# First norm reordered around its two modulation vectors, and the last two blocks of the recurrence gated one at a time

## The chip, the cores and the metric

The kernel runs on one core of one Trainium2 chip. The metric is the device time of one execution in microseconds (us). The core's engines are TensorE (PE in the profile; PEld is its weight load), VectorE (DVE), ScalarE (ACT), GpSimd (POOL) and SyncE (SP), which here only issues DMAs. The program is written engine by engine, each engine has its own instruction order, and semaphores are the only link between them.

## The reference, cut to what matters

Two stacks of layers run over 512 tokens of width 1024 in float32. The change touches two places: the norm and modulation in front of the first feed-forward block, and the end of the one recurrent block.

```python
def sublayer_input(x, g, mod_j):
    shift, scale, gate = mod_j[:, 0], mod_j[:, 1], mod_j[:, 2]
    h = rmsnorm(x, g) * (1 + scale[:, None, :]) + shift[:, None, :]
    return h, (1 + gate)[:, None, :]
...
    c_act = jax.nn.silu(c)
    for layer in range(DEPTH):
        mod = (c_act @ mod_w[layer] + mod_b[layer]).reshape(B, N_SUB, 3, D_MODEL)
        h, g = sublayer_input(x, norm_g[layer, 0], mod[:, 0])
        x = x + MACARON_W * g * swiglu(h, ffn_w_gu[layer, 0], ffn_w_down[layer, 0])
...
    a = jnp.exp(log_a)
    b = jnp.sqrt(-jnp.expm1(2.0 * log_a)) * (i * xc).astype(jnp.float32)
    _, hs = lax.associative_scan(_lin_rec_combine, (a, b), axis=1)
    y = jax.nn.gelu(gate) * hs.astype(h.dtype)
    return y @ w_out
```

The recurrence has 10 blocks of 128 channels, numbered 0 to 9.

## The kernel before, in words

Activations lie transposed, as `xT` with 8 tiles of 128 channels by 512 tokens. Every float32 product is made of three products of a high and a low part (`COMBOS`), so each weight panel of 128x2048 is loaded raw by a DMA, cast to its high part by ACT (`split_to`, L1385), and its low part is subtracted by DVE (L1953), or by POOL (L2675) for a few panels that are marked so. For the first feed-forward block, stage `f0`, the low part of the gate panel (panel 0) is made by DVE and that of the up panel (panel 1) by POOL. POOL waits for the step `gain f0` before it makes its first one.

**The start of the program.** One DMA queue brings, in this order, `c`, two pieces of `mod_w`, `x` in two halves, two more pieces of `mod_w`, the small tables, four more pieces of `mod_w`, and then the raw weight panels. A piece of `mod_w` is 256 rows of one of the vectors shift (part 0) or scale (part 1); four pieces make a part. `first_sums` multiplies the rows of a piece on DVE with the matching values of silu(c) and adds them, two instructions a piece, into a 128x1024 sum. `first_turn` sums it over its 128 partitions on TensorE: 8 products of 128x128 by one column of ones (L740), each of them two instructions in the trace, since the operands are float32. `biased` adds `mod_b` and evicts the vector (L1941), `gains` makes the gain of the norm out of the scale vector (L1992). Meanwhile TensorE transposes `x` (L1344), ACT copies it to `xT` (L1889) and then squares the token rows with their sums (L1894), `first_spread` on DVE makes 1/rms and puts it on diagonals (L2048), and `broadcast` (L776) spreads it over all partitions of two PSUM banks.

Then `apply` makes the input of the products, for each half h of the tokens and each of 8 channel tiles j: DVE `scaled` (L2115) writes a PSUM tile of bank 0 or 1, ACT makes `h_high` (L1436) with the shift as its bias, DVE makes `h_low` (L2125) in `rest`. `first_products` of TensorE (L806) follows tile by tile.

**Two helpers decide who waits.** `take_pair` hands out PSUM banks in pairs and first waits until whatever `free_pair` noted for the pair is done. A pair number is fixed if `only[0]` is set; otherwise the pairs go round: 0 for `c`, 2, 4, 6, 0 for `x`, 2 for the tables, 4 for the first call of `first_turn`. `fence` waits until all four engines have passed a mark:

```python
        def fence(q, name):
            for engine in ENGINES:
                q.wait_ge(*at("past", name, engine))
...
            def free_pair(b, *done):
                free[b] = free[b + 1] = list(done)
```

`scaled` holds `fence(q, ("norm", name))`. For `f0` the mark of TensorE is set right behind the second `first_turn`, so it stands for the end of that call. `first_bank("f0", 1)` is bank 4, and `norm_bank("f0", h)` are banks 6 and 7.

**The end of the recurrence.** For each pair of blocks DVE makes the input and two scans (L2333, one a block), POOL multiplies both blocks by gelu(gate) in one instruction of 128x1024 (L2742), ACT casts y_high block by block (L1454) and DVE subtracts y_low (L2152). `project_back` of TensorE then runs the panels of `lru_w_out`, 256 columns each; in the first of them blocks 8 and 9 are the last two of 8, with 6 matmuls of 512 columns each. The next panel's high part is cast by ACT behind its last y_high, and its low part is made by DVE behind that.

Of the kernel before, what the change touches and what calls it, by code (L numbers as in the profile page):

```python
# [9 lines left out]
ALU = mybir.AluOpType  # L10
# [3 lines left out]
P = 128  # L14
# [41 lines left out]
def build(nc, t, out):  # L56
    S, D = t["x"].shape[1:]
    KD = D // P
# [16 lines left out]
    with ExitStack() as ctx:  # L75
# [33 lines left out]
        with nc.sbuf_tensor("before_parts", [P, 12 * S], F32), nc.sbuf_tensor("sb_parts", [P, 4, TRI], F32R) as sb_parts:  # L109
# [18 lines left out]
        s_c, s_in, s_tab, s_rope, s_swap, s_out, s_gate_w, s_dup = (sem(n) for n in (  # L128
            "c_loaded", "x_loaded", "tables_loaded", "rope_loaded", "swapped", "stored", "gate_w_loaded", "copied_half"))
# [158 lines left out]

        entries = []
# [89 lines left out]
        first_acc = [mod_acc[:, :], tiles(20 * S, D)]  # L379
# [242 lines left out]
        def tensor(q):  # L622
# [113 lines left out]
            def first_turn(part):  # L736
                b = base_of["mod", 0, 0, part] = take_pair()
                q.wait_ge(*at("first_sum", part))
                for j in range(KD):
                    m = e.matmul(psum[:, b, j:j + 1], first_acc[part][:, j * P:(j + 1) * P], ones[:, 0:1], start=True, stop=True)  # L740
                m.then_inc(*q.up(s_sums, "mod_turned", 0, 0, part))
                free_pair(b, ("mod", 0, 0, part))
# [596 lines left out]
            q.wait_ge(*at("x_in"))  # L1339
# [33 lines left out]
        def scalar(q):  # L1373
# [53 lines left out]
            def apply(name, h, j0=0, j1=KD):  # L1427
                for j in range(j0, j1):
                    hs, tmp = HALF[h], scaled_tile(name, j)
                    q.wait_ge(*at("scaled", name, h, j))  # L1430
                    h_free(q, name, h)
                    shift = shift_of(name, j)
                    if shift is None:
                        e.copy(H[0][:, j, hs], tmp).then_inc(*q.up(s_square, "h_high", name, j, h))  # L1434
                    else:
                        e.activation(H[0][:, j, hs], tmp, ACT.Identity, bias=shift).then_inc(*q.up(s_square, "h_high", name, j, h))  # L1436
# [158 lines left out]
            def rglru():  # L1595
# [297 lines left out]
            for n in range(NT):  # L1893
                e.activation(row_squares[:, n, :], x_rows[:, n, :], ACT.Square, accum_out=row_sums[:, n:n + 1]).then_inc(*q.up(s_act, "row_square", n))  # L1894
            q.wait_ge(*at("vec_turned"))
            e.copy(vec[:, KD:n_vec], psum[:, base_of.get("vec", 0), 0:n_vec - KD]).then_inc(*q.up(s_act, "vec"))
            load_sqrt("f0")
            mean, root = (stats[0][:, 4 * i:4 * i + NT] for i in range(2))
            q.wait_ge(*at("norm_mean", "f0", 0, 0))
            e.activation(root, mean, ACT.Sqrt).then_inc(*q.up(s_square, "norm_root", "f0", 0, 0))  # L1900
# [14 lines left out]
        def vector(q):  # L1915
# [3 lines left out]
            def first_sums(part, kp):  # L1919
                q.wait_ge(*at("first_mods", part * KD // 2 + kp))  # L1920
                q.wait_ge(*at("c_act"))
                acc = first_acc[part]
                for k in range(2):
                    w, c = first_mods[part * KD // 2 + kp][:, k * D:(k + 1) * D], v("c_act", 2 * kp + k)
                    if kp == 0 and k == 0:
# [58 lines left out]
            def gains(name):  # L1984
                if name not in MOD_OF:
                    return
                layer, sub, weight = MOD_OF[name]
                m, o = mods[layer], 3 * sub * KD
                q.wait_ge(*at("mod", layer, sub, 0))
# [47 lines left out]

            def first_spread():

                mean, root, y2 = (stats[0][:, 4 * i:4 * i + NT] for i in range(3))  # L2040
                q.wait_ge(*at("row_square", NT - 1))
                e.tensor_scalar(mean, row_sums, 1.0 / D, EPS, ALU.mult, ALU.add).then_inc(*q.up(s_norm, "norm_mean", "f0", 0, 0))
# [47 lines left out]
            def apply(name, h, j0=0, j1=KD):  # L2090
# [27 lines left out]
                def rest(j):  # L2118
# [5 lines left out]
                    else:  # L2124
                        m = e.scalar_tensor_tensor(H[1][:, j, hs], scaled_tile(name, j), shift, high, ALU.add, ALU.subtract)  # L2125
# [179 lines left out]
            def rglru():  # L2305
# [21 lines left out]
                def scan(n0):  # L2327
# [338 lines left out]
        def gpsimd(q):  # L2666
# [66 lines left out]
            def rglru():  # L2733
                stage = "lru"

                def second(n0):
                    q.wait_ge(*at("lru_is", n0 + 1))
                    q.wait_ge(*at("conv", n0 + 1))
                    e.tensor_tensor(lru_ii, lru_ii, lru_xc[n0 // 2 % 2], ALU.mult).then_inc(*q.up(s_pool, "lru_ix", n0))
                    q.wait_ge(*at("lru_scan", n0 + 1))  # L2740
                    q.wait_ge(*at("gelu", n0))
                    e.tensor_tensor(lru_rr, lru_rr, lru_gelu[n0 // 2 % 2], ALU.mult).then_inc(*q.up(s_pool, "lru_gated", n0))  # L2742
# [148 lines left out]
        def sync(q):  # L2891
# [132 lines left out]
            def load_first(i):  # L3024
                e.dma_start(first_mods[i].rearrange("p (k n) -> p k n", k=2), mod_piece(i)[3]).then_inc(*q.up(s_first[i], "first_mods", i, by=16))
# [4 lines left out]
            for n in range(NT // 2):  # L3030
                e.dma_start(x_rows[:, 2 * n:2 * n + 2, :], t["x"][0, 2 * n * P:(2 * n + 2) * P, :].rearrange("(n p) d -> p n d", p=P)).then_inc(
                    *q.up(s_in, "x_in", by=16))
# [96 lines left out]
```

## Time and profile before

| what | value |
|---|---|
| three runs | 3153.94, 3156.24, 3156.54 us |
| median | 3156.24 us |
| profiled execution, its own time | 3154.35 us |
| its span | 3152.5 us |
| granted TensorE clock over the span | 0.988 of full |
| TensorE busy | 3076.4 us (98%) |
| VectorE, ScalarE, GpSimd busy | 1710.2, 1190.4, 253.2 us |

The span runs from the first to the last instruction of the profiled execution; its own time has 1.85 us more around it. Busy shares are averages over the whole program, and what one place is worth is read from the stretch around it.

### The profile page before, as it was taken

How to read it: one execution, taken by the hardware profiler on the slowest of the kernel's cores; microseconds unless marked ns; L12 is line 12 of the kernel's file. 1: busy time of each engine (PE TensorE's matmuls, PEld its weight loads, DVE VectorE, ACT ScalarE, POOL GpSimd, SP SyncE). 2: the span in 40 equal slices, each digit the busy share in tenths (PEclk: the TensorE clock that was granted, in tenths of full speed). 3: DMA queues.
4: the chain of work that ended last, by engine and by line, in shares of the span. 5: the costliest groups of instructions: out<-in, count | busy, mean ns of one | idle time of the engine just before them, and what ended most of it. 6: DMA issues, size and time to landing. Idle time of an engine off the chain costs nothing.

```text
span 3152.5 us, 38812 instructions
## 1 busy us (share of the span) xinstructions
PE 3076.4 (98%) x16353; PEld 2590.4 (82%) x16353; DVE 1710.2 (54%) x2365; ACT 1190.4 (38%) x1573; POOL 253.2 (8%) x324
## 2 busy tenths in 40 slices
PE   6999999999999999999999999899999999999998
PEld 6888898888888988888788888877777897787788
DVE  6555553245555554326764233569864356986434
ACT  4222246543222322224753132334573233457322
POOL 0000011120000000000210000012220001222000
PEclk8999999999999999999999999999999999999999
DMA  6545421114546353323122232242322224232222
GB/s 235 187 171 195 169 94 54 54 58 148 195 165 208 108 174 128 100 84 114 57 97 94 97 104 87 64 118 83 91 81 80 96 82 122 80 91 81 80 94 74
DMA packets 290150, 354.23 MB, mean 112 GB/s; under 512 B 10506, under 2 KB 264250, under 8 KB 289978
## 3 DMA queue, kind: packets, MB, share of 16 engines
q1 hardware_dynamic: 289978, 351.76, 34.0%
q8 instruction: 130, 2.13, 0.3%
q14 instruction: 42, 0.34, 0.0%
HBM read 336.52 MB, written 2.10 MB: 107 GB/s over the span
## 4 chain that ended last, share of the span: by engine, by line
PE 88%; DVE 7%; ACT 3%; DMA 1%; issue 1%; SPq 0%; POOL 0%; DVEq 0%; ACTq 0%; POOLq 0%
PE psum L689 53%; PE psum L1236 9%; PE psum L848 6%; PE psum L806 3%; PE psum L1327 3%; PE psum L710 2%; PE psum L730 1%; PE psum L946 1%; DVE w_low L1953 1%; DVE psum L2115 1%; PE psum L1154 1%; PE psum L1175 1%; PE psum L655 1%; DVE h_low L2125 1%; PE psum L802 1%
## 5 line engine op out<-in xcount | busy, mean ns | idle before, releaser
L689 PE MATMUL psum<-h_high,w_high 128*128 128x512 f32 (+1 forms) x1936 | 756.6, 391 | 0.6 <-DVE area L2632 0.4
L689 PE MATMUL psum<-h_high,w_low 128*128 128x512 f32 (+1 forms) x1936 | 753.5, 389 | 0.0
L689 PE MATMUL psum<-h_low,w_high 128*128 128x512 f32 (+1 forms) x1936 | 753.4, 389 | 0.0
L1953 DVE TENSOR_TENSOR w_low<-raw,w_high 128x2048 fp32r<-128x2048 f32 (+3 forms) x246 | 547.2, 2235 | 308.6 <-ACT w_high L1385 308.5
L1385 ACT CAST w_high<-raw 128x2048 fp32r<-128x2048 f32 (+4 forms) x254 | 464.6, 1843 | 570.4 <-DMA raw<-in_ffn_w_gu 234.3
L689 PEld LDWEIGHTS psum<-h_high,w_high 128*128 128x128 f32 (+1 forms) x1936 | 362.7, 187 | 79.8 <-ACT area L1708 1.8
L689 PEld LDWEIGHTS psum<-h_high,w_low 128*128 128x128 f32 (+1 forms) x1936 | 362.6, 187 | 76.6
L689 PEld LDWEIGHTS psum<-h_low,w_high 128*128 128x128 f32 (+1 forms) x1936 | 362.7, 187 | 76.2 <-issue 1.0
L2238 DVE TENSOR_TENSOR area<-area,psum 128x512 f32<-128x512 f32 x88 | 60.2, 684 | 340.5 <-PE psum L689 332.2
L689 PE MATMUL psum<-y_high,w_high 128*128 128x512 f32 x592 | 232.4, 393 | 5.6 <-DVE y_low L2152 3.7
L689 PE MATMUL psum<-y_high,w_low 128*128 128x512 f32 x592 | 231.1, 390 | 0.0
L689 PE MATMUL psum<-y_low,w_high 128*128 128x512 f32 x592 | 231.1, 390 | 0.0
L1454 ACT CAST y_high<-area 128x512 fp32r<-128x512 f32 x102 | 62.7, 620 | 435.3 <-DVE area L2238 404.1
L2157 DVE SCALAR_TENSOR_TENSOR xT<-psum,gain_out,xT 128x512 f32<-128x512 f32 (+1 forms) x156 | 90.7, 623 | 196.2 <-PE psum L689 158.0
L1236 PE MATMUL psum<-h_high,w_high 128*128 128x512 f32 x464 | 186.5, 402 | 3.5 <-ACT area L1768 3.5
L1236 PE MATMUL psum<-h_high,w_low 128*128 128x512 f32 x464 | 181.9, 392 | 0.0
L1236 PE MATMUL psum<-h_low,w_high 128*128 128x512 f32 x464 | 181.8, 392 | 0.0
L2675 POOL TENSOR_TENSOR w_low<-raw,w_high 128x2048 fp32r<-128x2048 f32 x8 | 37.0, 4620 | 1789.8 <-ACT w_high L1385 1750.0
L1970 DVE SCALAR_TENSOR_TENSOR mod_acc<-raw,vec,mod_acc 128x1024 f32<-128x1024 f32 x112 | 143.9, 1285 | 59.0 <-DMA raw<-in_mod_w 53.8
L806 PE MATMUL psum<-h_high,w_high 128*128 128x256 f32 x448 | 132.9, 297 | 7.1 <-ACT h_high L1434 2.2
L848 PE MATMUL psum<-y_high,w_high 128*128 128x256 f32 x480 | 138.2, 288 | 0.2
L848 PE MATMUL psum<-y_low,w_high 128*128 128x256 f32 x480 | 136.5, 284 | 0.0
(329 smaller groups left out, 5135.7 us busy)
## 6 DMA issues: line engine op xcount, KB each, us to landing
raw<-in_ffn_w_gu SPq DMA_DIRECT2D x88, 1024.0 KB, 5.8
raw<-in_mod_w SPq DMA_DIRECT2D x64, 1024.0 KB, 4.8
raw<-in_w_in SPq DMA_DIRECT2D x64, 1024.0 KB, 5.2
raw<-in_ffn_w_down SPq DMA_DIRECT2D x32, 1024.0 KB, 7.3
raw<-in_ffn_w_down SPq DMA_DIRECT2D x16, 768.0 KB, 4.8
raw<-in_sb_w_qkv SPq DMA_DIRECT2D x12, 1024.0 KB, 5.1
raw<-in_lru_w_in SPq DMA_DIRECT2D x10, 1024.0 KB, 5.1
raw<-in_w_out SPq DMA_DIRECT2D x8, 1024.0 KB, 5.2
```

The source lines that it names most:

```text
L689: mm = e.matmul(psum[0:width, base + m, :], wv[a][:, at_k, c0:c0 + width], X[b][:, k, :], start=(at_k == 0 and (a, b) == (0, 0)), stop=(at ...
L710: mm = e.matmul(psum[:, base + m, :], wv[a][:, at_k, m * P:(m + 1) * P], X[b][:, k, :], start=(at_k == 0 and (a, b) == COMBOS[0]), stop=(a ...
L806: mm = e.matmul(psum[:, base + m, HALF[h]], wv[a][:, k, m * P:(m + 1) * P], H[b][:, k, HALF[h]], start=first, stop=last)
L848: mm = e.matmul(psum[:, bank, m * S // 2:(m + 1) * S // 2], wv[a][:, at_k, m * P:(m + 1) * P], X[b][:, k, HALF[h]], start=(at_k == 0 and ( ...
L1236: mm = e.matmul(psum[:, bank, :], wv[a][:, k, m * P:(m + 1) * P], H[b][:, k, :], start=first, stop=last)
L1327: mm = e.matmul(psum[:, base + m, :], wv[x][:, k, m * P:(m + 1) * P], Y[y][:, k, :], start=(k == k0 and (x, y) == (0, 0)), stop=(k == k1 - ...
L1385: e.copy(w_high[x % NW][:, :n], raw[raw_at[m]][:, :n]).then_inc(*q.up(s_high, "w_high", x))
L1454: e.copy(Y[0][:, k, :], src).then_inc(*q.up(s_act, "y_high", stage, j))
L1953: e.tensor_tensor(w_low[raw_at[m]][:, :n], raw[raw_at[m]][:, :n], w_high[x % NW][:, :n].bitcast(F32), ALU.subtract).then_inc(*q.up(s_low, ...
L1970: g = e.scalar_tensor_tensor(mod_acc[:, :], w, c, mod_acc[:, :], ALU.mult, ALU.add)
L2157: return e.scalar_tensor_tensor(dst, src, gain_out[:, j:j + 1], dst, ALU.mult, ALU.add)
L2238: e.tensor_tensor(ffn_gated[n % 4], ffn_silu[n % 4], taken_product(up)[:, m, :], ALU.mult).then_inc(*q.up(s_vec, "gated", stage, n))
```

## The change

It has two halves. In the first norm, `FIRST_PARTS = (1, 0)` makes the scale part come first in the loads and sums. ACT squares the token rows before it copies the transposed `x`, with a semaphore of its own for each half of `x`. The first piece of the shift part is no longer summed by DVE: TensorE multiplies its 128x128 blocks directly with silu(c), and the summed rest is added in the same PSUM columns. The broadcasts of 1/rms are issued inside the second `first_turn`, between that piece and the rest. The shift takes bank 4 in place of bank 0. `biased` of the scale moves behind the shift sums, and DVE makes the low part of panel 0 and the shift vector inside `apply`, behind the first two `scaled`. In the recurrence, for blocks 8 and 9 alone, POOL gates block 8 behind its own scan and DVE gates block 9 behind the second scan.

```diff
+        FIRST_PARTS = (1, 0)
...
-        first_acc = [mod_acc[:, :], tiles(20 * S, D)]
+        first_acc = {FIRST_PARTS[0]: mod_acc[:, :], FIRST_PARTS[1]: tiles(20 * S, D)}
...
             def first_turn(part):
                 b = base_of["mod", 0, 0, part] = take_pair()
+                if part == FIRST_PARTS[1]:
+
+                    q.wait_ge(*at("first_mods", KD // 2))
+                    q.wait_ge(*at("c_act"))
+                    for k in range(2):
+                        for j in range(KD):
+                            e.matmul(psum[:, b, j:j + 1], first_mods[KD // 2][:, k * D + j * P:k * D + (j + 1) * P], v("c_act", k), start=(k, j) == (0, 0), stop=False,
+                                     skip_group_check=True)
+                    for h in range(2):
+                        broadcast("f0", h)
                 q.wait_ge(*at("first_sum", part))
                 for j in range(KD):
-                    m = e.matmul(psum[:, b, j:j + 1], first_acc[part][:, j * P:(j + 1) * P], ones[:, 0:1], start=True, stop=True)
+                    m = e.matmul(psum[:, b, j:j + 1], first_acc[part][:, j * P:(j + 1) * P], ones[:, 0:1], start=part == FIRST_PARTS[0], stop=True,
+                                 skip_group_check=True)
...
-            first_turn(0)
+            first_turn(FIRST_PARTS[0])
             for h in range(2):
-                b = norm_bank("f0", h)
-                wait_free(b)
-                broadcast("f0", h)
-            only[0] = 0
-            first_turn(1)
+                wait_free(norm_bank("f0", h))
+            only[0] = first_bank("f0", 1)
+            first_turn(FIRST_PARTS[1])
             only[0] = None
             q.mark("past", ("norm", "f0"), "PE")
...
-                        split_high(stage, n, n % KD, lru_rr[:, m, :], ("lru_gated", n0))
+                        split_high(stage, n, n % KD, lru_rr[:, m, :], ("lru_gated", n))
...
+            for n in range(NT):
+                q.wait_ge(*at("x_in", n // 2))
+                e.activation(row_squares[:, n, :], x_rows[:, n, :], ACT.Square, accum_out=row_sums[:, n:n + 1]).then_inc(*q.up(s_act, "row_square", n))
+            load_sqrt("f0")
+            mean, root = (stats[0][:, 4 * i:4 * i + NT] for i in range(2))
+            q.wait_ge(*at("norm_mean", "f0", 0, 0))
+            e.activation(root, mean, ACT.Sqrt).then_inc(*q.up(s_square, "norm_root", "f0", 0, 0))
             for j in range(1, KD, 2):
                 q.wait_ge(*at("x_turned", j))
...
-                    return [("mod", 0, 0, 1)]
+                    return [("mod", 0, 0, FIRST_PARTS[0])]
...
                 scaled(j0)
+                if (name, h) == ("f0", 0):
+                    scaled(j0 + 1)
+                    split_to(0)
+                    biased(0, 0, FIRST_PARTS[1])
                 for j in range(j0, j1):
                     if j + 1 < j1:
-                        scaled(j + 1)
+                        if (name, h, j) != ("f0", 0, 0):
+                            scaled(j + 1)
...
+                    if n0 == NB - 2:
+                        q.wait_ge(*q.newest)
+                        q.wait_ge(*at("gelu", n0))
+                        e.tensor_tensor(lru_rr[:, 1, :], lru_rr[:, 1, :], lru_gelu[n0 // 2 % 2][:, 1, :], ALU.mult).then_inc(
+                            *q.up(s_vec, "lru_gated", n0 + 1))
...
-            for part in range(2):
-                for kp in range(KD // 2):
-                    first_sums(part, kp)
-                    if (part, kp) == (1, 0):
-                        biased(0, 0, 0)
-                        first_spread()
-            split_to(0)
-            biased(0, 0, 1)
+            gain_part, shift_part = FIRST_PARTS
+            for kp in range(KD // 2):
+                if kp == 3:
+                    first_mean()
+                first_sums(gain_part, kp)
+            first_spread()
+            for kp in range(1, KD // 2):
+                first_sums(shift_part, kp)
+            biased(0, 0, gain_part)
             gains("f0")
             q.mark("past", ("norm", "f0"), "DVE")
             ffn("f0")
...
+                    q.wait_ge(*at("gelu", n0))
+                    if n0 == NB - 2:
+                        q.wait_ge(*at("lru_scan", n0))
+                        e.tensor_tensor(lru_rr[:, 0, :], lru_rr[:, 0, :], lru_gelu[n0 // 2 % 2][:, 0, :], ALU.mult).then_inc(*q.up(s_pool, "lru_gated", n0))
+                        return
                     q.wait_ge(*at("lru_scan", n0 + 1))
```

Left out of the diff are the two semaphores of the halves of `x`, the waits for them, the mean split off `first_spread` as `first_mean`, and the index arithmetic that follows `FIRST_PARTS`. ACT and DVE also wait for the shift vector in `apply` of every modulated norm, where `gains` waited for it before.

## Rows read from the trace of the kernel before

**Rows 1.** The page, part 1: busy time, share of the span, instructions.
```profile
PE 3076.4 (98%) x16353; PEld 2590.4 (82%) x16353; DVE 1710.2 (54%) x2365; ACT 1190.4 (38%) x1573; POOL 253.2 (8%) x324
```
**Rows 2.** The chain that ended last, 0 to 60 us: start, duration, what.
```profile
43.18 16.85 PE psum L806 x125
```
**Rows 3.** The timeline, 0 to 50 us: start, duration, engine, line, what, idle before.
```profile
13.76 6.53 PE L1344 MATMUL psum<-ident,area 128*128 128x128 f32 x32 [11.19 <-DMA area<-in_x]
...
16.30 5.31 DVE L1929 SCALAR_TENSOR_TENSOR mod_acc<-h_plain,vec,mod_acc 128x1024 f32<-128x1024 f32 x4 [5.07 <-DMA h_plain<-in_mod_w]
...
21.23 1.06 ACT L1894 ACTIVATE area<-area 128x1024 f32<-128x1024 f32 x1
...
22.79 0.75 DVE L1926 TENSOR_SCALAR area<-y_plain,vec 128x1024 f32<-128x1024 f32 x1 [1.17 <-DMA y_plain<-in_mod_w]
...
28.93 2.04 PE L776 MATMUL psum<-inv,ones 128*128 128x256 f32 x4 [4.74 <-DVE inv L2048]
29.29 8.03 DVE L1929 SCALAR_TENSOR_TENSOR area<-y_plain,vec,area 128x1024 f32<-128x1024 f32 x6
...
33.48 1.90 ACT L1385 CAST w_high<-raw 128x2048 fp32r<-128x2048 f32 x1 [5.63 <-DMA raw<-in_ffn_w_gu]
...
37.23 2.28 DVE L1953 TENSOR_TENSOR w_low<-raw,w_high 128x2048 fp32r<-128x2048 f32 x1
...
41.04 0.17 DVE L1941 TENSOR_TENSOR mod<-psum,vec 128x8 f32<-128x8 f32 x1 [1.53 <-PE psum L740]
...
41.52 0.88 DVE L2115 SCALAR_TENSOR_TENSOR psum<-xT,gain_in,psum 128x256 f32<-128x256 f32 x2
41.57 4.55 POOL L2675 TENSOR_TENSOR w_low<-raw,w_high 128x2048 fp32r<-128x2048 f32 x1 [39.79 <-DVE gain_in L1992]
42.05 0.87 ACT L1436 ACTIVATE h_high<-psum,mod 128x256 fp32r<-128x256 f32 x2 [3.65 <-DVE psum L2115]
42.55 0.48 DVE L2125 SCALAR_TENSOR_TENSOR h_low<-psum,mod,h_high 128x256 fp32r<-128x256 f32 x1
```
**Rows 4.** Line L740: count, ns min/median/max, first to last start in us.
```profile
L740 PE MATMUL psum<-ones,mod_acc x16: 242/250/352, 21.8 to 23.8; 128*128 128x1 f32 x16
L740 PE MATMUL psum<-ones,area x16: 344/352/353, 37.5 to 40.7; 128*128 128x1 f32 x16
```
**Rows 5.** TensorE by window: length, busy (instructions), granted clock, DMA share, GB/s.
```profile
23.00:23.50 0.50, 0.50 (x5) 0.50 1.15 467
...
38.00:40.00 2.00, 2.00 (x11) 0.50 1.08 386
...
46.00:47.00 1.00, 1.00 (x7) 0.56 0.07 16
...
1613.00:1614.00 1.00, 0.65 (x2) 0.80 0.00 0
```
**Rows 6.** The timeline by engine, 1505 to 1520 us: POOL and DVE.
```profile
1512.32 2.39 POOL L2742 TENSOR_TENSOR area<-area 128x1024 f32<-128x1024 f32 x1 [10.21 <-DVE area L2333]
...
1512.71 4.15 DVE L1953 TENSOR_TENSOR w_low<-raw,w_high 128x2048 fp32r<-128x2048 f32 x1 [0.47 <-ACT w_high L1385]
```
**Rows 7.** The timeline by engine, 1590 to 1640 us: DVE, POOL, ACT, DVE, DVE, PE, PE.
```profile
1607.02 2.34 DVE L2333 TENSOR_TENSOR_SCAN area<-area 128x512 f32<-128x512 f32 x2
...
1609.44 2.34 POOL L2742 TENSOR_TENSOR area<-area 128x1024 f32<-128x1024 f32 x1 [11.68 <-DVE area L2333]
...
1611.86 1.14 ACT L1454 CAST y_high<-area 128x512 fp32r<-128x512 f32 x2 [6.22 <-POOL area L2742]
...
1612.51 1.29 DVE L2152 TENSOR_TENSOR y_low<-area,y_high 128x512 fp32r<-128x512 f32 x2 [3.15 <-ACT y_high L1454]
...
1615.06 4.49 DVE L1953 TENSOR_TENSOR w_low<-raw,w_high 128x2048 fp32r<-128x2048 f32 x2 [1.17 <-ACT w_high L1385]
...
1613.35 0.55 PE L689 MATMUL psum<-y_high,w_high 128*128 128x512 f32 x1 [3.73 <-DVE y_low L2152]
...
1617.78 0.28 PE L848 MATMUL psum<-y_high,w_high 128*128 128x256 f32 x1
```

More of the change, by code:

```diff
@@ L127, in build @@
         s_first = [sem(f"first_mods{i}") for i in range(KD)]
-        s_c, s_in, s_tab, s_rope, s_swap, s_out, s_gate_w, s_dup = (sem(n) for n in (
-            "c_loaded", "x_loaded", "tables_loaded", "rope_loaded", "swapped", "stored", "gate_w_loaded", "copied_half"))
+        s_in = [sem(f"x_loaded{i}") for i in range(NT // 2)]
+        s_c, s_tab, s_rope, s_swap, s_out, s_gate_w, s_dup = (sem(n) for n in (
+            "c_loaded", "tables_loaded", "rope_loaded", "swapped", "stored", "gate_w_loaded", "copied_half"))
         steps, base_of = {}, {}
@@ L1338, in tensor @@
             turn_tables(0, 1, "c_vec")
-            q.wait_ge(*at("x_in"))
+            for n in range(NT // 2):
+                q.wait_ge(*at("x_in", n))
             for j in range(KD):
@@ L1435, in apply @@
                     else:
+                        q.wait_ge(*at("mod", *MOD_OF[name][:2], 0))
                         e.activation(H[0][:, j, hs], tmp, ACT.Identity, bias=shift).then_inc(*q.up(s_square, "h_high", name, j, h))
@@ L1892, in scalar @@
                     q.mark("x", "f0", jj, 1)
-            for n in range(NT):
-                e.activation(row_squares[:, n, :], x_rows[:, n, :], ACT.Square, accum_out=row_sums[:, n:n + 1]).then_inc(*q.up(s_act, "row_square", n))
             q.wait_ge(*at("vec_turned"))
             e.copy(vec[:, KD:n_vec], psum[:, base_of.get("vec", 0), 0:n_vec - KD]).then_inc(*q.up(s_act, "vec"))
[L1897 to L1900, printed above, removed]
             for i, a in enumerate((neg_tri, neg_ones)):
@@ L1919, in first_sums @@
             def first_sums(part, kp):
-                q.wait_ge(*at("first_mods", part * KD // 2 + kp))
+                i = FIRST_PARTS.index(part) * KD // 2 + kp
+                q.wait_ge(*at("first_mods", i))
                 q.wait_ge(*at("c_act"))
@@ L1923, in first_sums @@
                 for k in range(2):
-                    w, c = first_mods[part * KD // 2 + kp][:, k * D:(k + 1) * D], v("c_act", 2 * kp + k)
-                    if kp == 0 and k == 0:
+                    w, c = first_mods[i][:, k * D:(k + 1) * D], v("c_act", 2 * kp + k)
+                    if kp == FIRST_PARTS.index(part) and k == 0:
                         m = e.tensor_scalar(acc, w, c, None, ALU.mult)
@@ L1988, in gains @@
                 m, o = mods[layer], 3 * sub * KD
-                q.wait_ge(*at("mod", layer, sub, 0))
                 q.wait_ge(*at("mod", layer, sub, 1))
@@ L2036, in spread, with first_mean @@
                     m.then_inc(*q.up(s_norm, "norm_diag", name, h, which))
+            def first_mean():
+                mean = stats[0][:, 0:NT]
+                q.wait_ge(*at("row_square", NT - 1))
+                e.tensor_scalar(mean, row_sums, 1.0 / D, EPS, ALU.mult, ALU.add).then_inc(*q.up(s_norm, "norm_mean", "f0", 0, 0))
             def first_spread():
                 mean, root, y2 = (stats[0][:, 4 * i:4 * i + NT] for i in range(3))
-                q.wait_ge(*at("row_square", NT - 1))
-                e.tensor_scalar(mean, row_sums, 1.0 / D, EPS, ALU.mult, ALU.add).then_inc(*q.up(s_norm, "norm_mean", "f0", 0, 0))
                 q.wait_ge(*at("norm_root", "f0", 0, 0))
@@ L2124, in rest @@
                     else:
+                        q.wait_ge(*at("mod", *MOD_OF[name][:2], 0))
                         m = e.scalar_tensor_tensor(H[1][:, j, hs], scaled_tile(name, j), shift, high, ALU.add, ALU.subtract)
@@ L2739, in second @@
                     e.tensor_tensor(lru_ii, lru_ii, lru_xc[n0 // 2 % 2], ALU.mult).then_inc(*q.up(s_pool, "lru_ix", n0))
+                    q.wait_ge(*at("gelu", n0))
[3 more added lines that the diff above has]
+                        return
                     q.wait_ge(*at("lru_scan", n0 + 1))
-                    q.wait_ge(*at("gelu", n0))
-                    e.tensor_tensor(lru_rr, lru_rr, lru_gelu[n0 // 2 % 2], ALU.mult).then_inc(*q.up(s_pool, "lru_gated", n0))
+                    e.tensor_tensor(lru_rr, lru_rr, lru_gelu[n0 // 2 % 2], ALU.mult).then_inc(*q.up(s_pool))
+                    for m in range(2):
+                        q.mark("lru_gated", n0 + m)
                 first_products(stage)
@@ L3024, in load_first @@
             def load_first(i):
-                e.dma_start(first_mods[i].rearrange("p (k n) -> p k n", k=2), mod_piece(i)[3]).then_inc(*q.up(s_first[i], "first_mods", i, by=16))
+                src = mod_piece(FIRST_PARTS[2 * i // KD] * KD // 2 + i % (KD // 2))[3]
+                e.dma_start(first_mods[i].rearrange("p (k n) -> p k n", k=2), src).then_inc(*q.up(s_first[i], "first_mods", i, by=16))
             e.dma_start(t_rows[0:KD, 0, :], t["c"].rearrange("a (n p) -> (a n) p", p=P)).then_inc(*q.up(s_c, "c_in", by=16))
@@ L3031, in sync @@
                 e.dma_start(x_rows[:, 2 * n:2 * n + 2, :], t["x"][0, 2 * n * P:(2 * n + 2) * P, :].rearrange("(n p) d -> p n d", p=P)).then_inc(
-                    *q.up(s_in, "x_in", by=16))
+                    *q.up(s_in[n], "x_in", n, by=16))
             load_first(2)
```

## The prediction, made before the changed kernel ran

> **What bounds the kernel now.** I read the page first: TensorE is busy for 98% of the span [rows 1]. A start of about 43 us and a handful of stalls are all that an edit to the other engines can win, and every microsecond by which TensorE begins its steady work later is a microsecond at the end. Next the chain that ended last, in its first 60 us: the products of stage `f0` enter it at 43.18 and run on without a gap [rows 2]. So the first half of the change is worth whatever it moves that one time by. The timeline shows what ends last there [rows 3]: the shift and scale sums on DVE stop at 37.32, TensorE turns the second vector until 41.0 [rows 4], DVE evicts it at 41.04, scales two tiles from 41.52, and ACT and DVE finish the first h tile at 43.03. The second half of the change touches one stall of 3.73 us, behind the last two blocks of the recurrence [rows 7].
>
> **First half, the sums.** The order of the loads does not change, only which part the pieces hold. The transposes begin at 13.76, when both halves of `x` are there, and a square of 128x1024 takes 1.06 with some 0.2 for its sum, so four end by about 18.7 even if they start only then. The third and fourth piece's sums run from 16.30 to 21.61 [rows 3]. The mean fits between them, the root is ready when they end, and the spread of 1/rms is over by about 23.5. The xT copies come some 2 us later than before, at about 23.4, and nobody asks for them before 40 us. Before, `first_spread` sat in the middle of the shift sums, waiting for ACT, and six sums ran from 29.29 to 37.32 [rows 3]. Now only the loads hold them. The fifth piece landed at 22.79 and the raw gate panel, four loads later, at 33.48 [rows 3], so a load takes 2.67 and the last piece lands at about 30.8. Its two sums of 1.3 each end at 33.4, 3.9 us earlier than before. That is the gain of this half.
>
> **First half, what stands in front of TensorE.** The second `first_turn` begins with `take_pair`. With `only[0]` at `first_bank("f0", 1)` it asks for bank 4, and bank 4 is the one that the round of pairs gave to the scale vector, noted as free when the scale vector is evicted. DVE evicts it (`biased`) only behind all its shift sums, at 33.6. So the product of the first shift piece and the two broadcasts, which are meant to fill the idle TensorE from 24 us on, stand in the queue until 33.7. No row shows banks; this is read from the code.
>
> What then runs on TensorE: the piece has 16 products of a 128x128 block by one column, 32 instructions. In the same form 16 instructions started over 37.5 to 40.7 [rows 4], 0.215 each, so 32 take 6.9, to 40.6. The two broadcasts took 2.04 [rows 3] and end at about 42.6. The turn of the rest is the old 16 instructions, 3.5 [rows 4], and ends at 46.1.
>
> DVE meanwhile has nothing to do. Its next instruction is `scaled`, whose fence asks for TensorE's mark of this norm, and the mark is still set behind the second `first_turn`. So both `scaled` wait until 46.1, not for the broadcast alone. They take 0.88, and then comes `split_to(0)`, the low part of panel 0, 2.28 [rows 3], which before ran at 37.23 beside the turn of the vector and cost nothing. That cover is gone: 46.15 to 47.05, and to 49.35. The shift vector with its small gaps makes 49.6, h_high (0.48) 50.1, h_low (0.48) 50.6, and with the old step of 0.15 to TensorE the first product starts at 50.75, against 43.18 [rows 2]. **The first half costs 7.5 us.** Behind ACT's first h_high stand only the other h_high; behind DVE's wait stand all its low parts, and TensorE waits for both. POOL's low part of the up panel is freed earlier (its wait for the gain ends at 33.8, before at 41.5) and is needed only after 48 products, so it gives nothing. After the start the pace is that of before: h tiles every 0.91 us on DVE, TensorE at half clock at first. From 60 us on TensorE waits for little, and what the DMA queue does next hangs on TensorE's own marks, so I carry the 7.5 to the end.
>
> **The clock in this stretch.** The granted clock was 0.50 (1.2 GHz) from 23.0, in the middle of the first one-column products, through all of the second ones, and rose at about 46.7, some 3.6 us into the dense products of `f0` [rows 5]. So 3.5 us of one-column products did not raise it, and it even fell during such products. I take half clock for all 48 of the new run.
>
> The Trainium skill (TensorE: Matmul & The Clock Gate, Part 1) says that an idle array is clocked at half, and that sustained activity gives the full clock back. It makes no exception for one-column products. By that rule TensorE, busy from 33.7 for 12 us, would be at full clock for most of them. The case that this gives is the second rival.
>
> **Second half, the recurrence.** Before: two scans to 1609.36, POOL's gate of both blocks to 1611.78, y_high of block 8 to 1612.45, y_low of block 8 to 1613.16, TensorE at 1613.35 [rows 7]. Now POOL has half the work, 1.17, and DVE the other half, some 0.68 by its y_low of the same size [rows 7]. POOL could start at 1608.2, behind the first scan. But the second scan runs then, on two SBUF operands. In the one place where such an operation of DVE was issued beside POOL's gate, it took 4.15 in place of 2.28, and ended one normal duration behind POOL's end [rows 6, 3]. So I take the two engines as excluding one another: POOL gates from 1609.4 to 1610.6, DVE's gate of block 9 runs behind it to 1611.25, y_high of block 8 is ready at 1611.2, y_low from 1611.3 to 1611.95, TensorE at 1612.15, 1.2 earlier. The next panel's low part comes 1.15 earlier too (ACT's casts follow its last y_high, 1611.85 against 1613.0), and with it the start at 1617.78 [rows 7]. After its stall of 3.73 TensorE ran at half clock (0.80 granted in the window in which it resumed [rows 5]). With 2.5 us of idle time it may keep the full one for its 12 matmuls, but it would then wait for that low part, so little more comes of it: **1.3 us gained**. Bounds: with no exclusion POOL is done at 1609.4, DVE at 1610.1, y_low of block 8 at 1610.8, and 2.6 are gained. If DVE's gate goes first, POOL ends at 1611.3 and 0.5 are gained.
>
> The Trainium skill (GPSIMD Engine Reference, Key points) states that GpSimd shares its SBUF interfaces with VectorE, and that they contend when the DVE instruction has two SBUF inputs. Rows 6 agree with it. For a scan no row here shows it; without the rule's reach to scans the gain would be nearer 2.6.
>
> **The sum.** +7.5 − 1.3 = +6.2 us. The profiled execution took 3154.35, its span 3152.5 with 1.85 around it, which gives 3160.6. It lies 1.9 below the median of the three runs, 3156.24, and from the median it is 3162.4. I forecast 3162. The nearest runs before lie up to 2.6 us apart, so about 0.2%, 6.3 us, is what a measurement of this kernel can tell from no change, and the forecast lies on that line.
>
> **The rivals.**
>
> 1. *The piece runs early after all*: TensorE is not held at bank 4. For it: it is what the new order is built for, and my reading of the round of pairs has no row behind it. Then the first vector is turned by 24.2, the piece by 31.0, the broadcasts by 33.0, the rest from 33.5 to 37.1, which is 9.0 earlier than in my case. The first half gives −1.5 (the low part of panel 0 and the fence remain), the total is −2.8 us: 3153.4, no slower than before. It decides if the first of the 32 instructions starts before DVE's eviction of the scale. 0.10.
>
> 2. *The long run on TensorE raises the clock*. Against it stand rows 5. The first 3.5 us at half clock hold 16 instructions, to 37.2, the next 16 at half the spacing 1.7, the broadcasts 1.0, the turn 1.75, to 41.7: 4.4 earlier, the first half costs 3.1, the total is +1.8: 3158. 0.13.
>
> 3. *The recurrence gives nothing*: a gate of half the size costs POOL as much as the whole, 2.34 [rows 7], and block 8 is as late as before. Against it: POOL's 128x2048 took 4.55 and its 128x1024 2.34 [rows 3, 7], so it goes by size. The total is then +7.4: 3163.6, slower by 0.23%. It decides as soon as POOL's half takes over 2.2. 0.12.
>
> Something else 0.05; my own case 0.60.
>
> **The numbers.** My case alone: the landing of the last piece may be off by 1 either way, the turn by 0.5, the recurrence is between −2.6 and −0.5, so +4.5 to +8.3, that is 3160.5 to 3164.5. The range for all cases takes in rivals 2 and 3, most of the scatter of the runs and part of rival 1: 3155 to 3165.5. Slower by over 0.2% are nearly half of my case (0.29), most of rival 3 (0.10) and a little of the rest: 0.41. Faster by over 0.2% needs −6.3, which no case gives: 0.03. Within 0.2%: 0.56.
>
> **What would show it.** Right: L740's new 32 instructions start at about 33.7, released by DVE, and the clock stays 0.50; DVE is idle from 34 to 46; its w_low of panel 0 starts at about 47; the first L806 at about 50.7; POOL's gate of block 8 starts at 1.2 to 1.3 us behind the first scan (1609.4 plus the shift), DVE's own gate behind it. Wrong: L740's new instructions at 24 us (rival 1), a clock of 1.00 before 42 us (rival 2), `scaled` before the end of the turn (then I misread the fence, and 3 to 4 us of the cost go), or a later stage whose stall takes the shift up.

## The result, and the profile after

The changed kernel took 3164.01 us (median of ten runs, 3161.4 to 3167.3), the kernel before 3156.59 (ten runs beside it): ratio 1.0024, 95% interval 1.0015 to 1.0033, so it is 0.24% slower, 7.4 us. I had forecast 3162, in a range of 3155 to 3165.5, with 0.41 on slower by over 0.2%. The profiled execution took 3161.87 with a span of 3160.1, against 3154.35 and 3152.5. Line numbers shift by some 13 to 30: L740 is now L752, the new shift piece is L746, L776 is L789, L806 is L819, L1953 is L1968, L2115 is L2132, L2742 is L2772.

The chain that ended last, in its part of the first 60 us, beside [rows 2]:

```profile
24.09 9.56 issue
33.66 6.96 PE psum L746 x32
40.62 1.92 PE psum L789 x4
42.53 3.22 PE psum L752 x16
...
45.94 0.88 DVE psum L2132 x2
46.82 2.19 DVE w_low L1968
...
50.34 11.77 PE psum L819 x77
```

The products of `f0` begin at 50.34 where they began at 43.18. Before them, three blocks of TensorE work stand nose to tail, and before those a hole of 9.56 us. The profile calls it "issue" and names no releaser. By the code, the first thing that TensorE's queue asks for there is the wait in `take_pair` for bank 4, and the bank 2 run below tests that. The timeline of the changed kernel has both sides of the hole, and beside [rows 3] it shows what ran earlier:

```profile
11.52 1.06 ACT L1901 ACTIVATE area<-area 128x1024 f32<-128x1024 f32 x1 [7.24 <-DMA area<-in_x]
...
28.17 5.31 DVE L1944 SCALAR_TENSOR_TENSOR area<-y_plain,vec,area 128x1024 f32<-128x1024 f32 x4 [0.47 <-DMA y_plain<-in_mod_w]
...
33.40 0.16 DVE L1956 TENSOR_TENSOR mod<-psum,vec 128x8 f32<-128x8 f32 x1
...
33.66 6.96 PE L746 MATMUL psum<-vec,y_plain 128*128 128x1 f32 x32 [9.56 <-issue]
...
38.83 4.50 POOL L2704 TENSOR_TENSOR w_low<-raw,w_high 128x2048 fp32r<-128x2048 f32 x1 [37.05 <-ACT w_high L1397]
...
45.94 0.88 DVE L2132 SCALAR_TENSOR_TENSOR psum<-xT,gain_in,psum 128x256 f32<-128x256 f32 x2 [12.19 <-PE psum L752]
46.73 2.28 DVE L1968 TENSOR_TENSOR w_low<-raw,w_high 128x2048 fp32r<-128x2048 f32 x1
```

The sums end at 33.48 instead of 37.32. The shift piece starts 0.1 us behind the end of DVE's eviction of the scale (33.40 and 0.16). DVE is idle for 12.19 us, until the turn (L752) ends. TensorE by window, columns as in [rows 5]:

```profile
34.00:36.00 2.00, 2.00 (x11) 0.50 1.10 347
...
44.00:46.00 2.00, 1.74 (x9) 0.50 0.01 2
...
54.00:56.00 2.00, 2.00 (x13) 0.60 0.00 0
56.00:57.00 1.00, 1.00 (x11) 1.00 0.00 0
```

TensorE is busy from 33.66 to 45.75, all of it at half clock, and the clock rises only at about 55.6, 5.3 us into the dense products, where it took 3.7 before (to 46.9).

The end of the recurrence, beside [rows 7], in the order of the engines DVE, POOL, ACT, PE:

```profile
1614.48 2.34 DVE L2356 TENSOR_TENSOR_SCAN area<-area 128x512 f32<-128x512 f32 x2
1616.86 1.59 DVE L2361 TENSOR_TENSOR area<-area 128x512 f32<-128x512 f32 x1
1618.64 1.29 DVE L2175 TENSOR_TENSOR y_low<-area,y_high 128x512 fp32r<-128x512 f32 x2 [0.19 <-ACT y_high L1467]
...
1621.20 4.49 DVE L1968 TENSOR_TENSOR w_low<-raw,w_high 128x2048 fp32r<-128x2048 f32 x2 [1.19 <-ACT w_high L1397]
...
1615.85 2.05 POOL L2772 TENSOR_TENSOR area<-area 128x512 f32<-128x512 f32 x1 [9.91 <-DVE area L2356]
...
1619.48 0.47 PE L691 MATMUL psum<-y_high,w_high 128*128 128x512 f32 x1 [1.72 <-DVE y_low L2175]
...
1623.64 0.35 PE L861 MATMUL psum<-y_high,w_high 128*128 128x256 f32 x1 [1.19 <-DVE w_low L1968]
```

POOL's half began at 1615.85, behind the first scan, but ended at 1617.90: 1.08 behind the end of the second scan at 1616.82. That start is not the one that I had named as a sign, some 1.2 us behind the end of the first scan. The profile has the instruction as begun and shows the wait inside its 2.05 us, where half of POOL's 2.34 for both blocks would be 1.17. DVE's own gate needed 1.59 in place of some 0.68, and ended 0.55 behind POOL. So the end times say that the two engines took turns. The stall in front of block 8 is 1.72 instead of 3.73, and a new wait of 1.19 for the low part of the next panel follows.

For the lags and leads below I counted the matmuls of two traces back from the last one and compared the starts of matmuls with the same count; a lag says how much later, a lead how much earlier a version does the same work than the kernel before, each in its profiled execution. In the changed kernel the lag behind the kernel before is 7.2 us at the start of `f0`, 7.8 from 60 us on, 8.1 in front of block 8, 5.9 at the next panel, 6.0 at 1900 us, up to 9.2 behind 2000 us, and 7.5 at the end.

### The profile page after: what moved, and what is told of

It reads as the page before. It is cut to its first block, busy times and chain, and to the rows that moved or that the text cites. A ratio compares the mean times of both kernels' runs of the same rounds, so it can differ in the third digit from the quotient of the medians.

```text
span 3160.1 us, 38877 instructions
## 1 busy us (share of the span) xinstructions
PE 3080.6 (97%) x16385; PEld 2595.5 (82%) x16385; DVE 1707.1 (54%) x2364; ACT 1189.8 (38%) x1573; POOL 253.7 (8%) x324
## 4 chain that ended last, share of the span: by engine, by line
PE 87%; DVE 7%; ACT 3%; issue 1%; DMA 1%; SPq 0%; POOL 0%; DVEq 0%; ACTq 0%; POOLq 0%
PE psum L691 53%; PE psum L1249 9%; PE psum L861 6%; PE psum L819 3%; PE psum L1340 3%; PE psum L712 2%; PE psum L732 1%; PE psum L959 1%; DVE w_low L1968 1%; DVE psum L2132 1%; PE psum L1167 1%; PE psum L1188 1%; PE psum L657 1%; DVE h_low L2143 1%; PE psum L815 1%
## 5 line engine op out<-in xcount | busy, mean ns | idle before, releaser
L1968 DVE TENSOR_TENSOR w_low<-raw,w_high 128x2048 fp32r<-128x2048 f32 (+3 forms) x246 | 547.3, 2236 | 309.7 <-ACT w_high L1397 309.7
L1985 DVE SCALAR_TENSOR_TENSOR mod_acc<-raw,vec,mod_acc 128x1024 f32<-128x1024 f32 x112 | 143.8, 1284 | 60.8 <-DMA raw<-in_mod_w 55.6
L819 PE MATMUL psum<-h_high,w_high 128*128 128x256 f32 x448 | 132.9, 297 | 10.4 <-DVE h_low L2143 4.6
```

The lines of the kernel that those rows point to most:

```text
L819: mm = e.matmul(psum[:, base + m, HALF[h]], wv[a][:, k, m * P:(m + 1) * P], H[b][:, k, HALF[h]], start=first, stop=last)
L1968: e.tensor_tensor(w_low[raw_at[m]][:, :n], raw[raw_at[m]][:, :n], w_high[x % NW][:, :n].bitcast(F32), ALU.subtract).then_inc(*q.up(s_low, ...
L1985: g = e.scalar_tensor_tensor(mod_acc[:, :], w, c, mod_acc[:, :], ALU.mult, ALU.add)
```

## The experiments

All are compared with the kernel before, run on the same chip beside them (median 3155.27, then 3155.11).

| run | median, us | runs | ratio, 95% interval | first product of `f0`, us |
|---|---|---|---|---|
| norm_only | 3163.92 | 5 | 1.0032 (1.0020 to 1.0044) | 50.44 |
| recur_only | 3153.82 | 12 | 0.9995 (0.9987 to 1.0004) | 43.49 |
| bank2 | 3155.61 | 11 | 1.0003 (0.9994 to 1.0011) | 42.18 |
| bank2_mark | 3153.91 | 11 | 0.9995 (0.9987 to 1.0004) | 40.48 |
| no_panel | 3158.23 | 10 | 1.0008 (0.9999 to 1.0018) | 47.11 |
| mark_only | 3162.40 | 10 | 1.0020 (1.0011 to 1.0029) | 47.52 |
| warm | 3151.28 | 11 | 0.9983 (0.9974 to 0.9992) | 40.40 |
| best | 3149.78 | 11 | 0.9986 (0.9978 to 0.9995) | 40.52 |

**The first half alone.** The edit puts the recurrence back:

```diff
-                        split_high(stage, n, n % KD, lru_rr[:, m, :], ("lru_gated", n))
+                        split_high(stage, n, n % KD, lru_rr[:, m, :], ("lru_gated", n0))
...
-                    if n0 == NB - 2:
-                        q.wait_ge(*q.newest)
-                        q.wait_ge(*at("gelu", n0))
-                        e.tensor_tensor(lru_rr[:, 1, :], lru_rr[:, 1, :], lru_gelu[n0 // 2 % 2][:, 1, :], ALU.mult).then_inc(
-                            *q.up(s_vec, "lru_gated", n0 + 1))
```

> The first half of the change alone, the recurrence as before. My account: the whole loss is here. First product of f0 at about 50.3 us against 43.2, the stall in front of block 8 of the recurrence back at 3.7 us, the time 7 to 8 us above before. Rival (the loss comes from both halves or from later stages): well under 5 us above before.

It took 8.7 us more than before (6.3 to 13.9 by the interval, from five runs), a little above the 7 to 8 that I expected. The lag is 7.3 at the start of `f0`, 7.4 behind it and 7.0 at 1618. The loss is all in this half. POOL's gate and TensorE behind it:

```profile
1616.46 2.36 POOL L2766 TENSOR_TENSOR area<-area 128x1024 f32<-128x1024 f32 x1 [11.01 <-DVE area L2356]
...
1620.39 0.47 PE L691 MATMUL psum<-y_high,w_high 128*128 128x512 f32 x1 [3.12 <-DVE y_low L2175]
```

The stall is 3.12 here, not 3.7: the first half moved TensorE by 7.7 and DVE only by 7.0 at this point (the scans start at 1614.04 against 1607.02), and the difference came off the stall.

**The second half alone**, the same lines put into the kernel before:

> The second half alone, the first norm as before. My account: POOL's gate of block 8 and DVE's of block 9 exclude each other as in the changed kernel, the stall shrinks from 3.7 to about 2.4 us, full clock behind it, 1.5 to 2.3 us below before; that is under what the time can show, so the trace has to. Rival (the gain of 2.2 us seen in the changed kernel was there only because the first half had shifted TensorE against DVE): 0.5 us or less at the first product of the next panel.

```profile
1608.42 2.04 POOL L2748 TENSOR_TENSOR area<-area 128x512 f32<-128x512 f32 x1 [10.36 <-DVE area L2333]
...
1612.04 0.47 PE L689 MATMUL psum<-y_high,w_high 128*128 128x512 f32 x1 [2.12 <-DVE y_low L2152]
1616.19 0.36 PE L848 MATMUL psum<-y_high,w_high 128*128 128x256 f32 x1 [1.14 <-DVE w_low L1953]
```

TensorE resumes at 1612.04 instead of 1613.35 and reaches the next panel at 1616.19 instead of 1617.78. TensorE ran 0.3 us late before that point, so against its own lag it gained 1.6 and 1.9 us. DVE was not late (its scans start at 1607.05 against 1607.02), and counted from the start of the scans TensorE resumes 1.3 us earlier and reaches the next panel 1.6 us earlier. In the changed kernel the same count gives 1.3 and 1.6 too. So 1.6 of the 2.3 seen there are the half's own and independent of the first half; the rest is the shift between DVE and TensorE seen in norm_only, of which this run has 0.3. The time itself (1.45 us below before) can't tell this from nothing. The rival falls.

**The shift vector in bank 2**, one argument:

```diff
-            only[0] = first_bank("f0", 1)
+            only[0] = first_bank("f0", 0)
```

> The changed kernel with the shift vector in bank 2 in place of bank 4, nothing else. My account: nothing holds the shift piece any more, its 32 instructions start at about 24 to 26 us, the broadcasts end before 33.4, the turn of the rest ends at about 37, both scaled follow at once (the fence still waits for the turn), low part of panel 0 to 40.2, first product at about 41.5: some 9 us earlier than in the changed kernel, 1.5 earlier than before, time some 3 to 4 us below before. Rival (the 32 instructions on TensorE are themselves the cost): first product still behind 48 us.

```profile
24.09 5.82 PE L746 MATMUL psum<-vec,y_plain 128*128 128x1 f32 x32
...
29.77 2.05 PE L789 MATMUL psum<-inv,ones 128*128 128x256 f32 x4
...
37.78 0.88 DVE L2132 SCALAR_TENSOR_TENSOR psum<-xT,gain_in,psum 128x256 f32<-128x256 f32 x2 [3.56 <-PE psum L752]
38.57 2.28 DVE L1968 TENSOR_TENSOR w_low<-raw,w_high 128x2048 fp32r<-128x2048 f32 x1
39.33 5.93 POOL L2704 TENSOR_TENSOR w_low<-raw,w_high 128x2048 fp32r<-128x2048 f32 x1 [37.55 <-ACT w_high L1397]
...
42.18 0.55 PE L819 MATMUL psum<-h_high,w_high 128*128 128x256 f32 x1 [4.61 <-DVE h_low L2143]
```

The same 32 instructions now start at 24.09, and the hole is gone. The first product comes 8.2 us earlier than in the changed kernel. I expected 41.5; in this execution DVE's last sum ended 0.46 later, at 33.94. So bank 4 is the cause of the hole, and the shift piece does not hold up the first product where it stands in TensorE's idle time. `scaled` still waits for the turn (3.56 idle, released by PE). The time is back at that of before and not 3 to 4 below it: the lead is 2.9 us behind the recurrence and turns into a lag of 1.3 by the end. More on that below.

**The mark moved behind the broadcasts**, on top of bank 2:

```diff
                     for h in range(2):
                         broadcast("f0", h)
+                    q.mark("past", ("norm", "f0"), "PE")
...
             only[0] = None
-            q.mark("past", ("norm", "f0"), "PE")
```

> As the bank 2 version, and TensorE's mark of the norm set behind the broadcasts instead of behind the turn of the rest. My account: both scaled start at about 33.7, the low part of panel 0 runs from 35.7 (its high part) to 38.0 beside the turn, ACT's cast of panel 1 ends at 38.7 and holds the first h_high, first product at about 39.8, 1.7 earlier than with the bank alone, time 5 to 6 us below before. Rival (the mark changes nothing, since the shift vector is awaited anyway): first product within 0.5 us of the bank 2 version.

```profile
36.07 0.88 DVE L2132 SCALAR_TENSOR_TENSOR psum<-xT,gain_in,psum 128x256 f32<-128x256 f32 x2 [2.27 <-ACT w_high L1397]
36.86 2.28 DVE L1968 TENSOR_TENSOR w_low<-raw,w_high 128x2048 fp32r<-128x2048 f32 x1
...
40.48 0.55 PE L820 MATMUL psum<-h_high,w_high 128*128 128x256 f32 x1 [3.33 <-DVE h_low L2143]
```

The step was right, 1.7 us between the two versions as expected, but for the size by luck: `scaled` started not at 33.7 but at 36.07, released by ACT's cast of panel 0. ACT has a mark of its own in the same fence, set behind its first `split_to`, which I had not looked at. The lead behind the recurrence is 6.0 us (1.3 of it from a stretch near 450 us in which the clock fell before and did not here), the lead in the medians 1.4, where I had expected 5 to 6.

**The mark alone, with bank 4 kept:**

> The changed kernel with bank 4 kept and only the mark moved behind the broadcasts. My account: the shift piece still starts at 33.7, both scaled start at 42.5 when the broadcast is done, the low part of panel 0 waits for POOL's panel 1 (to 43.4) and ends at 45.6, the shift vector comes at 45.9, first product at about 47.1: 3.2 us earlier than in the changed kernel. Rival (the mark changes nothing, since the shift vector is awaited anyway): 50.

```profile
39.16 4.51 POOL L2704 TENSOR_TENSOR w_low<-raw,w_high 128x2048 fp32r<-128x2048 f32 x1 [37.38 <-ACT w_high L1397]
...
43.07 0.88 DVE L2132 SCALAR_TENSOR_TENSOR psum<-xT,gain_in,psum 128x256 f32<-128x256 f32 x2 [8.98 <-PE psum L790]
43.86 2.28 DVE L1968 TENSOR_TENSOR w_low<-raw,w_high 128x2048 fp32r<-128x2048 f32 x1
...
47.52 0.55 PE L820 MATMUL psum<-h_high,w_high 128*128 128x256 f32 x1 [1.46 <-DVE h_low L2143]
```

`scaled` is now released by the broadcast (L790) and no longer by the turn. The first product lies 2.8 us before that of the changed kernel, 3.2 expected, in an execution in which the shift piece itself started 0.33 late (33.99). Both of the waits that I read from the code are thus shown one by one. The median, 3162.40, is hardly below that of the changed kernel.

**No shift piece on TensorE**, all four pieces on DVE, bank and mark as in the changed kernel:

```diff
-                    q.wait_ge(*at("first_mods", KD // 2))
-                    q.wait_ge(*at("c_act"))
-                    for k in range(2):
-                        for j in range(KD):
-                            e.matmul(psum[:, b, j:j + 1], first_mods[KD // 2][:, k * D + j * P:k * D + (j + 1) * P], v("c_act", k), start=(k, j) == (0, 0), stop=False,
-                                     skip_group_check=True)
...
-            for kp in range(1, KD // 2):
+            for kp in range(KD // 2):
                 first_sums(shift_part, kp)
```

> The changed kernel (bank 4 and the mark as they are) with all four shift pieces summed on DVE and no shift piece on TensorE. DVE has 2 us free before the second shift piece lands, so its sums should still end at about 33.5. My account: the broadcasts start at 33.7 and end at 35.7, the turn ends at 39.1, both scaled follow; then DVE's low part of panel 0 meets POOL's of panel 1, which has run since 38.8. If two such instructions exclude each other it ends near 45.5 and the first product starts at about 47; if not, at 42.2 and 43.6. Rival (the order of the norm is the cost and not the queue in front of TensorE): first product at 50 as in the changed kernel.

```profile
34.12 2.05 PE L782 MATMUL psum<-inv,ones 128*128 128x256 f32 x4 [9.98 <-issue]
...
39.13 4.50 POOL L2697 TENSOR_TENSOR w_low<-raw,w_high 128x2048 fp32r<-128x2048 f32 x1 [37.35 <-ACT w_high L1390]
...
40.37 5.41 DVE L1961 TENSOR_TENSOR w_low<-raw,w_high 128x2048 fp32r<-128x2048 f32 x1
...
47.11 0.55 PE L812 MATMUL psum<-h_high,w_high 128*128 128x256 f32 x1 [7.73 <-DVE h_low L2136]
```

The hole stays without the piece, since the broadcasts stand behind the same wait. DVE's sums end at 33.94, in an execution whose raw panel came 0.3 late, so some 0.2 later than with the piece on TensorE if that is taken off: in the changed kernel DVE was idle for 2.00 us until the next piece landed, and an extra piece takes 2.03. So the shift piece on TensorE buys next to nothing, and in bank 4 it puts 6.9 us more in front of the turn. Only 3.2 of those come back at the first product, because DVE's low part then meets POOL's: 5.41 us for an instruction of 2.28, ending 2.15 behind POOL's end at 43.63. In the bank 2 run, where DVE's instruction came first, it is POOL that pays, 5.93 for 4.55.

**Four dense products in the gap**, on top of bank 2 and the moved mark:

```diff
                 free_pair(b, ("mod", 0, 0, part))
+                if part == FIRST_PARTS[1]:
+                    for i in range(4):
+                        e.matmul(psum[:, b + 1, 0:S // 2], ones[:, :], inv[:, 0:S // 2], start=True, stop=True)
```

> The version with bank 2 and the moved mark, with four extra dense products (128x128 by 256 columns of float32, result never read, no part of the reference's computation is left out) on TensorE behind the turn, in the gap of 3.3 us before the first product. My account: one-column products do not raise the clock and dense ones do, so with these four the clock rises within about 1 us of the first product where it took 3.5 us, the first 17 products run at full clock, and TensorE is then paced by DVE: up to 1.5 us gained behind the first panel half, first product itself at 40.5. Rival (TensorE's being busy is what counts, and it was busy from 24 to 37 in vain): no change of the rise.

Windows without them (first three lines) and with them (last three):

```profile
37.00:39.00 2.00, 0.15 (x1) 0.50 1.10 356
...
41.00:43.00 2.00, 2.00 (x12) 0.50 0.79 315
43.00:44.00 1.00, 1.00 (x6) 0.51 0.02 8
```

```profile
37.00:39.00 2.00, 2.00 (x6) 0.50 1.10 357
39.00:40.00 1.00, 1.00 (x3) 0.51 1.07 394
40.00:41.00 1.00, 0.99 (x7) 1.00 1.04 408
```

The clock rises at about 40.0, 0.4 us before the first product, against 44.0. In both versions TensorE ran the one-column products from 24.5 to 31.4 and from 33.5 to 37.1 and the two broadcasts between them at half clock, and the clock did not rise; with the four dense products behind them it rose 3.1 us after they began. In the run of the next experiment, with the same four products, it rose at about 41.8, 4.9 us after they began and 1.3 behind the first product, so their effect is there but not to the microsecond. The lead is 3.6 against 2.8 at 48 us, less than the 1.5 more that I allowed for, since TensorE now waits for DVE's tiles, and from 60 us on it is 3.3 against 2.8. The time is 3151.28, 0.17% below before. That these 0.5 us make the step from bank2_mark (3153.91) is not shown: the two intervals overlap.

**Casts before y_high in the recurrence**, on top of that:

```diff
+                split_to(beyond_back(stage, EARLY, 2))
                 out(NB - 2)
```

> As warm, and in the recurrence ACT casts the high parts of the two panels behind the last recurrence blocks before it casts y_high of blocks 8 and 9, in the 4 us in which it is idle. My account: the low part of the next panel on DVE follows y_low at once, 1.2 to 1.4 us earlier, and TensorE's wait for it (1.2 us in the changed kernel) goes. TensorE's resumption in front of block 8 stays. Rival (DVE's two panels were not the bound, ACT's y_high is delayed instead): the next panel no earlier. In time against before: 6 to 8 us less, if the later stages do not give it back as they did for the bank 2 and mark version.

```profile
1602.16 3.70 ACT L1400 CAST w_high<-raw 128x2048 fp32r<-128x2048 f32 x2
1607.07 1.17 ACT L1470 CAST y_high<-area 128x512 fp32r<-128x512 f32 x2 [1.21 <-POOL area L2776]
...
1609.02 4.49 DVE L1972 TENSOR_TENSOR w_low<-raw,w_high 128x2048 fp32r<-128x2048 f32 x2
```

The casts fill ACT's idle time, DVE's low parts follow y_low without a gap, and TensorE does not wait at the next panel: 3.5 us gained over the recurrence where warm gained 2.2, as expected. The time, 3149.78, is 0.14% below before (interval 0.05% to 0.22%, 1.6 to 6.9 us), so 6 to 8 us less did not come, and it can't be told from that of warm. It is the fastest median of all.

## Why the prediction came out as it did

**The waits in front of TensorE: right, both.** The start of the piece was 33.7 and 33.66 measured, the first product 50.75 and 50.34. Its terms: piece 6.9 and 6.96, end of the broadcasts about 42.6 and 42.5, end of the turn 46.1 and 45.75 (the three blocks overlap a little where I added them), low part of panel 0 on the path, 2.28. The bank 2 run removes the first wait (8.2 us at the first product, 9.0 in my first rival) and the mark run the second (2.8, where I had said 3 to 4). In the fence I overlooked ACT's mark; it decided nothing until the first two waits were gone.

**The clock at the start: half for all 48 instructions, right.** Rival 2 had full clock before 42 us; it is out, since every instruction from 33.66 to 45.75 ran at 0.50. I carried the +7.5 unchanged through the start of `f0`, though. The clock rose 5.3 us into the products and not 3.7 (my 3.6 was read a little early: 0.56 over 46 to 47 us puts the rise at 46.9), and the lag grew there from 7.2 to 7.8.

**The recurrence: the mechanism right, the size too small.** I gave it 1.3; it gave 1.9 alone and 2.3 in the changed kernel (lag 8.14 to 5.86). POOL and DVE did take turns, in the order I took (POOL first), and counted from the start of the scans TensorE resumed 1.3 us earlier, against 1.2, and the low part of the next panel began 1.3 earlier, against 1.15. The term that I sized too small is what full clock gives: before, the next panel began 0.43 behind the end of its low part, since TensorE, slowed by the half clock, was still busy, and now it begins 0.15 behind. That makes 1.6. The other 0.7 in the changed kernel is how much less the first half had delayed DVE (7.5) than TensorE (8.1) in front of block 8, a shift between two engines that my sum has no term for.

**The sum.** The lag was 7.8 behind the start of `f0`, grew by 0.3 up to block 8 and shrank by 2.3 there; it was +5.9 at the next panel and +6.0 at 1900 us, against my +6.2. That it came so close is in part luck: the loss was 0.6 larger than my 7.5, the gain 1.0 larger than my 1.3, and the two errors offset each other. The time showed +7.4. The difference of 1.5 arose behind 2000 us, where the code is the same; the profiled execution shows it too, 7.5 at the end. Rival 1 (the piece runs early) and rival 3 (the recurrence gives nothing) are out: the piece starts at 33.66, and block 8 comes earlier. The bank run is rival 1 made true, with a lead of 1.0 at the first product against the 1.5 worked out for it. POOL's half did take 2.05, near the 2.2 that was to decide for rival 3, but by the end times about half of it was waiting for the scan.

**What stays open: the last 1100 us.** My step "I carry the 7.5 to the end" holds for what is left of the 7.5 up to 2000 us, and not behind it. The bank 2 and mark version leads by 6.0 us there, and ends with a lead of 0.4 in its profile and 1.4 in the medians. One of the places, first before, then the bank 2 and mark version:

```profile
2083.34 8.60 PE L1084 MATMUL psum<-y_plain 64*128 64x128 f32 x32 [2.52 <-DMA y_plain<-y_plain]
```

```profile
2078.67 11.02 PE L1098 MATMUL psum<-y_plain 64*128 64x128 f32 x32 [3.96 <-DMA y_plain<-y_plain]
```

It is the same wait for the same small DMAs, but 2.52 in one and 3.96 in the other, and the 32 transposes behind it took 8.60 and 11.02. The granted clock in 2080 to 2090 was 0.83 and 0.57. Behind most such waits the clock falls for a few microseconds, but not behind all: near 450 us TensorE waits for 2.03 us in both, and it fell to 0.50 before and not in the bank 2 and mark version. The time of one and the same program also differs: before alone ran from 3150.2 to 3161.7. And the same lag does not cost the same. In their profiled executions no_panel and mark_only both lag by 3.0 us at 2000 us, with the same code from there on, but 7.9 and 5.5 at the end; in the medians it is the other way round, 3.1 and 7.3. That such falls happened, and that this place went so differently, is shown. That they are what took 3 to 5 us of the medians from the two bank 2 versions, and 1.5 from the changed kernel, is my reading, and not shown.

## What to carry to other kernels

When work is moved into an engine's idle time, read what its own queue asks for in front of it. Here a round of PSUM pairs handed out a bank whose eviction stood behind all of another engine's sums, and one argument of the bank's choice was worth 8 us at the first product. A mark that a fence waits for has to move with the last work that it protects, or it also waits for everything that was put in front of it. And ask first whether the work needs to move: DVE stood idle for 2.00 us when the shift piece was there, and its sums take 2.03, so the move gained some 0.2 us at best.

## What the runs showed that I had not expected

- A `tensor_tensor` of POOL and an operation of DVE with two SBUF operands excluded each other in the places shown here, whichever came first, scans too: DVE 5.41 for 2.28, POOL 5.93 for 4.55, DVE 1.59 for about 0.68, POOL 2.05 for about 1.17. DVE's `scaled`, with one operand in PSUM, ran beside POOL at its usual 0.88 in the no_panel run.
- 24 one-column products (48 instructions) and two broadcasts in a row, 12.1 us of busy TensorE, ran at half clock to the end; with four dense products of 256 columns in the gap, the clock rose 3.1 us after their start in one run and 4.9 us in the other.
- Between 2000 us and the end the lag against the kernel before changed by −1.4 to +7.0 us in the profiled executions, though the code there is the same in all versions. A gain of 3 to 6 us in this kernel has to be read from the stretch where it arises; the time does not carry it through.
